# New states leave by transfers of single values, in place of transposes on TensorE with a staging buffer

## The reference

```
xn = rms_norm(x);  h, Bg, Cg, u, ga, gb = split(xn @ w_in)
conv_y, new_conv = causal_dwconv3(Cg * h, conv_buf)          # 512 channels
ssm_y, new_re, new_im = s5_mimo(u, s_re, s_im, ...)          # 32 groups x 64 complex states
x = x + (sigmoid(ga) * z_a + sigmoid(gb) * z_b) @ w_o
up_a, up_b = split(rms_norm(x) @ w_up)
up_a, new_ffn = causal_dwconv3(up_a, ffn_buf)                # 2816 channels
x = x + (gelu(up_a) * up_b) @ w_down
x = x + sigmoid(rms_norm(x) @ w_ple_gate) * (p @ w_ple);  y = rms_norm(x)
```

## Time and profile before

| | us |
|---|---|
| median of three runs (1610.47 to 1613.06) | 1612.05 |
| profiled execution, its own time | 1611.67 |
| its span, first to last instruction | 1609.9 |
| TensorE busy | 1553.1 |
| VectorE busy | 729.8 |
| ScalarE busy | 409.5 |
| GpSimd busy | 365.3 |

### The profile page before, as it was taken

One profiled execution on the slowest core, in us unless ns is written; L12 is line 12 of the kernel. 1 busy time (PEld: TensorE's weight loads), 2 busy tenths in 40 slices (PEclk: granted clock), 3 DMA queues, 4 the chain that ended last, 5 costly groups with the idle time before them and its releaser, 6 DMA issues.

```text
span 1609.9 us, 23664 instructions
## 1 busy us (share of the span) xinstructions
PE 1553.1 (96%) x9919; PEld 1536.0 (95%) x9919; DVE 729.8 (45%) x769; ACT 409.5 (25%) x466; POOL 365.3 (23%) x156
## 2 busy tenths in 40 slices
PE   7999997899999999999999999999999999989997
PEld 6989997899999999999999999999999999987996
DVE  4896797122222222234353444534344353447344
ACT  6302211243422232233121121211211112045113
POOL 1121220121211223433112131221303213054110
PEclk9899998999999999999999999999999999999999
DMA  6633526432211113232021020210202111020003
GB/s 179 200 86 92 82 53 171 108 85 70 76 40 50 52 39 107 91 105 74 5 78 52 26 65 13 78 52 27 65 13 78 39 39 52 26 66 14 27 23 119
DMA packets 165601, 109.48 MB, mean 68 GB/s; under 512 B 18192, under 2 KB 157116, under 8 KB 165486
## 3 DMA queue, kind: packets, MB, share of 16 engines
q1 hardware_dynamic: 158898, 100.25, 22.3%
q10 hardware_dynamic: 6656, 8.57, 1.6%
HBM read 90.21 MB, written 17.51 MB: 67 GB/s over the span
## 4 chain that ended last, share of the span: by engine, by line
PE 84%; DVE 7%; issue 5%; ACT 2%; DMA 1%; POOL 0%; SPq 0%; ACTq 0%; DVEq 0%; POOLq 0%
PE PS L1514 62%; PE PS L1784 16%; PE PS L1727 2%; DMA WST<-in_w_in 1%; DVE XL L1098 1%; PE PS L1677 1%; PE PS L1564 1%; POOL WL L603 0%; DVE ST L1206 0%; DVE ST L1207 0%; DVE XT L1418 0%; DVE OUTT L1493 0%; DVE S L1208 0%; DVE Q L1152 0%; DVE S L1210 0%
## 5 line engine op out<-in xcount | busy, mean ns | idle before, releaser
L603 POOL TENSOR_TENSOR WL<-WST,WH 128x1024 fp32r<-128x1024 f32 x108 | 261.7, 2424 | 1085.6 <-ACT WH L680 1085.6
L1514 PE MATMUL PS<-XH,WH 128*128 128x344 f32 x1920 | 409.8, 322 | 9.4 <-DVE TA L1117 3.9
L1514 PE MATMUL PS<-XL,WH 128*128 128x344 f32 x1920 | 408.9, 321 | 0.0
L1514 PE MATMUL PS<-XH,WL 128*128 128x344 f32 x1920 | 406.1, 320 | 0.0
L1514 PEld LDWEIGHTS PS<-XH,WH 128*128 128x128 f32 x1920 | 323.4, 188 | 11.1 <-issue 9.1
L1514 PEld LDWEIGHTS PS<-XL,WH 128*128 128x128 f32 x1920 | 326.2, 190 | 0.0
L1514 PEld LDWEIGHTS PS<-XH,WL 128*128 128x128 f32 x1920 | 321.0, 188 | 0.0
L680 ACT ACTIVATE WH<-WST 128x1024 fp32r<-128x1024 f32 x108 | 110.3, 1021 | 323.4 <-PE PS L1514 228.2
L1418 DVE TENSOR_TENSOR XT<-PS,XT 128x1032 f32<-128x1032 f32 x88 | 108.2, 1230 | 82.7 <-PE PS L1784 82.7
L1784 PE MATMUL PS<-GH,DHW 128*128 128x344 f32 x528 | 113.1, 323 | 5.4 <-DVE GL L1412 4.4
L1784 PE MATMUL PS<-GL,DHW 128*128 128x344 f32 x528 | 112.4, 321 | 0.0
(11 more groups left out here) (270 smaller groups left out, 1738.1 us busy)
## 6 DMA issues: line engine op xcount, KB each, us to landing
WST<-in_w_up SPq DMA_DIRECT2D x44, 512.0 KB, 3.9
WST<-in_w_in SPq DMA_DIRECT2D x32, 512.0 KB, 4.4
DST<-in_w_down SPq DMA_DIRECT2D x11, 1024.0 KB, 5.1
xscr<-XT SPq DMA_DIRECT2D x1, 4128.0 KB, 15.0
WST<-in_w_o SPq DMA_DIRECT2D x8, 512.0 KB, 4.4
WST<-in_w_ple_gate SPq DMA_DIRECT2D x8, 512.0 KB, 4.0
out_y_prompt<-OUTT SPq DMA_DIRECT2D x8, 512.0 KB, 2.9
XN<-in_x_prompt ACTq DMA_DIRECT2D x6, 512.0 KB, 8.5
```

What stands on the lines that cost most here:

```text
L603: nc.gpsimd.tensor_tensor(WL[:, w], WST[:, slot, 0:tiles * P], WH[:, w].bitcast(F32), ALU.subtract).then_inc(s_wl, 1)
L1514: last = mm(PS[:, 3 * (n % 2) + c, 0:TN], ww[:, w], xx[:, cols], start=(k == 0 and r == 0), stop=(k == ks - 1 and r == 2))
```

## The change

The 15 turns, the staging buffers OST and SST and SP's ten stores go. ScalarE issues transfers straight from FS and LAST to the outputs. One transfer fills one row of an output (one part of one batch entry), with the columns of FS or LAST as the source, so that every element is a piece of 4 bytes. 18 for the SSM and 10 for convolution A, with one plain copy of old rows from input to output, are issued behind `rms(1, N_A0)`; 10 for the FFN and one plain copy behind `gelu(FT - 1)`. The last wait of SP counts 40 transfers in place of 10.

```diff
@@ SP
-            sp.wait_ge(s_mf, M_OUT + 15)
-            sp.dma_start(out["conv_a_p"][0, 0], OST[0:2, 0:CA]).then_inc(s_so, 16)
...
-                sp.dma_start(out[f"ssm_{part}_p"][0].rearrange("b g p -> b (g p)"), half[0:1, :]).then_inc(s_so, 16)
-                sp.dma_start(out[f"ssm_{part}_s"][0].rearrange("b g p -> b (g p)"), half[1:1 + NB, :]).then_inc(s_so, 16)
...
-            sp.wait_ge(s_so, 160)
+            sp.wait_ge(s_so, 16 * (2 * (NB + 1) + 2 * (NB + 3)))
@@ ScalarE
             hi(G_P6, G_P6 % 2, N_A0)
             rms(1, N_A0)
 
+            for c, part in enumerate(("re", "im")):
+                rows = [out[f"ssm_{part}_p"][0, 0]] + [out[f"ssm_{part}_s"][0, b] for b in range(NB)]
+                for b, row in enumerate(rows):
+                    act.dma_start(row.rearrange("(j two) p -> (two p) j", two=2), FS[:, c, :, b],
+                                  allow_slow_non_contiguous=True).then_inc(s_so, 16)
+
+            def conv_states_out(name, kept, first, end):
+                rows = [out[name + "_p"][0, 0, k] for k in range(2)] + [out[name + "_s"][0, b, 1] for b in range(NB)]
+                for b, row in enumerate(rows):
+                    act.dma_start(row.rearrange("(t p) -> p t", p=P), LAST[:, first:end, b],
+                                  allow_slow_non_contiguous=True).then_inc(s_so, 16)
+                act.dma_start(out[name + "_s"][0, :, 0, :], a[kept][0, :, 1, :]).then_inc(s_so, 16)
+
+            conv_states_out("conv_a", "state_conv_a", 0, CT)
+
...
             gelu(FT - 1)
+            conv_states_out("ffn", "state_ffn_conv", CT, CT + FT)
             act.wait_ge(s_dst, FP * 16 + 16)
...
             hi(G_P7L, 0, N_PW0)
-            for k in range(4):
-                states_out(k)
             rms(2, N_P7)
-            for k in range(4, 15):
-                states_out(k)
@@ TensorE
-            for k in range(4):
-                states_out(k)
             sum_squares(N_P7, 2 * DT + 1)
-            for k in range(4, 8):
-                states_out(k)
             rms_read(2)
...
             down_out(N_PW0, N_PW0, 0, PH, PL, PHW, PLW)
-            for k in range(8, 15):
-                states_out(k)
...
-            pe.wait_ge(s_mf, M_OUT + 15)
+            pe.wait_ge(s_mf, M_PT + 5)
```

More of the change, by code:

```diff
@@ L88 @@
 M_PT = M_YO(CT)
-M_OUT = M_PT + 5
 def _stage_count(g, i=None, per_trip=0):
@@ L165, in decoder_step @@
         PL = at("PL", [P, PT * T], B0 + 6 * TB4, F32R)
-        SST = at("SST", [NB + 1, 2 * NJ * P], B0)
         AP = at("AP", [NJ, NPOW, P], C0)
@@ L191, in decoder_step @@
         PLW = at("PLW", [P, 2 * D], C0 + 16384, F32R)
-        OST = at("OST", [NB + 2, CA + FF], C0)
         XT = at("XT", [P, DT * T], D0)
@@ L977, in _ @@
                 split_hi(None, tile(XT, m), m, KV[:, K_PLE + m:K_PLE + m + 1], TC, DT + m + 1)
[L979 to L984, removed]
             def ple_gate(m, n):
```

## The result

The changed kernel takes 1838.03 us (median of 4 runs, 1820.08 to 1845.29), the kernel before 1611.26 (4 runs, 1609.39 to 1613.06). The ratio is 1.139, 95% interval 1.1305 to 1.1477: slower by 226.8 us. The forecast was slower by 68, with 1617 to 1775 as its range: right in sign, wrong by a factor of 3.3 in size, and the measured time lies outside the range. The profiled execution of the changed kernel took 1834.31 us, its span 1832.4. Its four runs lie 25 us apart, those of the kernel before 4.

A forecast was written before the change was run, and what follows sets the result against it. TensorE, busy 96%, was taken to bound the kernel, so holding up its inputs costs time. Stalls of 41.4 and 26.6 plus 1.6 for the clock less 1.2 for the turns gave +68.4 us: 1680 us, range 1617 to 1775.

The forecast's parts named there:

- The places: ScalarE held after the square root at 711.25 and the GELU ending at 1427.9; TensorE stalls 41.4 and 26.6 us.
- cover: Time ScalarE can be held before TensorE stalls: 8.3 us at the first place, 5.8 at the second.
- The price of a piece: Each 4-byte piece of the state stores takes a DMA engine 20 ns; ends 11.7 and 56.
- the middle of US: Source of the 20 ns: the store of US, 32 B pieces to HBM, estimated at 7 to 34 ns each.
- second rival: Pieces dearer, as many engines write 4 B into one short run: 40 to 56 ns, 1762 to 1828 us; 22%.
- WC's 56 ns: Price per piece from the WC transfers, 117.5% of 160 us over 3353 packets; upper end for the price.
- US and BN: Evidence against dear pieces: US's 32 B store at 34 ns at most; BN's 2048 pieces of 64 B, issued in 511 ns.
- The depth of the queue: ScalarE's queue, taken to be like SP's, still holds 140 pieces per engine when the last issue ends.
- The turns: After the FFN, removing them starts the next product 2.8 us sooner; clock restart costs 1.6, net 1.2 us gained.
- Traffic: Small pieces share DMA engines with weight loads, but a load has a product's time in hand, so no cost.
- The final wait: At the kernel's end: free, last piece leaves by 1463 us, 147 us before the end; up to 100 ns per piece.

The follow-up runs named there:

- values apart: Changed kernel with the same 38 transfers at the same places, but every value goes to scratch 640 B from the next; 1687.38 us, ratio 1.0476.
- the trials: Two kernels that store no states; in their place ScalarE issues nine trials of four transfers each at the first place; 32 B pieces took 10 ns.
- trial 2: In the kernel pricing pieces, without state stores: 4-byte stores to scratch, each partition's 16 to a run of its own; 41.5 us, 76 ns per piece.
- trial 0: In the kernel pricing pieces, without state stores: 4-byte stores to neighbouring places of one scratch row, as in the change; 36.2 us, 65 ns per piece.
- trial 1: In the kernel pricing pieces, without state stores: the same 4-byte pieces stored to scratch, each 640 B from the next; 12.4 us, 19 ns per piece.
- the first kernel that spread the rows: Changed kernel with its 38 transfers issued one at a time by SP between weight loads, none by ScalarE; 1621.39 us, ratio 1.0067 to the kernel before.

## Why the prediction was wrong

**The places, right.** TensorE's two waits stand where they were named, on WL and on GL, and each equals ScalarE's idle time less cover. First place: 143.5 - 8.3 = 135.2, measured 135.2. Second: 92.4 - 5.8 = 86.6 more than the old 4.4, so 91.0; measured 94.5. The missing 3.5 us are new: PHW and the last split are held together, so GpSimd makes PLW (1654.73, 4.50 us) while VectorE makes GL. VectorE and GpSimd there:

```profile
1655.64 4.69 DVE L1402 TENSOR_TENSOR GL<-TC,GH 128x1032 fp32r<-128x1032 f32 x1 [88.58 <-ACT GH L665]
```

```profile
1654.73 4.50 POOL L650 TENSOR_TENSOR PLW<-DST,PHW 128x2048 fp32r<-128x2048 f32 x1 [98.19 <-ACT PHW L665]
```

The same instruction took 1.23 us before, and 4.69 beside GpSimd's.

**The price of a piece: the step that failed.** The sum had 20 ns, "the middle of US, since that is the one small store to HBM". The packets that moved on ScalarE's queue can be counted. Changed kernel, windows 706 to 850.6 and 850.6 to 880 us (first place held, and what was left), then 1559 to 1652.6 and 1652.6 to 1700 (second place):

```profile
q10 hardware_dynamic: 41736, 0.17, 112.2%
q10 hardware_dynamic: 712, 0.02, 16.6%
q10 hardware_dynamic: 28104, 0.11, 138.9%
q10 hardware_dynamic: 232, 0.09, 5.2%
```

In the 144.6 us of the first place 2608 packets moved per engine, in the 93.4 of the second 1756: 55 and 53 ns each. With the values apart, in windows 710 to 764.7 and 1473 to 1507.2:

```profile
q10 hardware_dynamic: 42185, 0.17, 102.2%
q10 hardware_dynamic: 28021, 0.11, 114.6%
```

That is 2637 in 53.8 us and 1751 in 34.2, 20 ns each, just the forecast's price; and that kernel took 1687 us against the 1680 of the forecast. So the rows behind the 20 ns were not wrong for values that lie apart. What they lacked was the address: neighbours in one row of an output. US writes runs of 32 B, and such pieces cost 10 ns in the trials, with gaps or without. The second rival had the right price ("many engines write 4 B each into the same short run of a row") and, with WC's 56 ns, 1828 us; it was given 22%, and the range ended at 1775, near that rival's lower end of 1762. The argument against it was taken from US and BN, neither of which writes single values side by side. Its many engines are not needed, as trial 2 shows.

**The depth of the queue: no fixed number of pieces.** 140 per engine were assumed to be left when the last issue ends. By the same count of packets, in which one counts when it starts, 138 were left in trial 0 and 211 in trial 1, but only 45 at the first place (712 packets) and 15 at the second (232), where the last issue is the plain copy. So almost nothing was taken off the holds. That is 95 and 125 pieces more than the forecast held ScalarE for, at 55 and 53 ns together 12 us of the miss. It is also why the kernel with its values apart came out 18 us above its own expectation, which had taken off 250 where 16 and 20 were left. The count says when ScalarE is free, not when the values are there: trial 0 had started its last packet by 740 us and landed at 747.

**The turns, right in the first term, low in the second.** 2.8 us sooner and 1.6 lost to the clock, 1.2 net, were forecast. Measured in the changed kernel: 2.7 and 2.5, 0.15 net; without any stores 2.7 and 1.9.

**Traffic, right, with a gap.** A load has a product's time in hand almost everywhere, but not at the start of the FFN, where the first kernel that spread the rows lost 11 us. In the changed kernel that place was safe, since the pieces were in ScalarE's queue and came later. The final wait was free, as forecast: the last pieces had moved by 1700 us of 1832. (The margin given for it, 100 ns a piece, is 84 by the forecast's own figures; nothing hangs on it, as the hold moves the end of the kernel too.)

Sum with the measured terms: 135.2 for WL, 1.5 for the restart behind it, 94.5 - 4.4 = 90.1 for GL, less 0.15: 226.6 us. The spans of the two profiled executions differ by 222.5 only, but the changed kernel began the first FFN product 4.5 us sooner (708.24 against 712.71), in a stretch that the change does not touch; from there on it is 227.0. That the medians differ by 226.8 as well is in part luck.

## What to carry to other kernels

Before a transfer is cut into single values, count the pieces per DMA engine and look at where they land: at equal count the same transfers cost the kernel three times as much when the values were neighbours in HBM (227 us against 77). An engine that issues many such transfers in a row stands still until nearly all have moved (15 and 45 pieces per engine were left here of 1760 and 2624), so such transfers go one by one, on an engine whose stream has nothing urgent behind them, and never ahead of a load that is due. And a gap that must be there anyway is a free place for work on TensorE: taking the work out let the clock fall here and gave back almost nothing.

## What the runs showed of the hardware that was not expected

- In one execution each of the two kernels with trials, a 4-byte store to HBM took 76 ns per piece and engine with the next one 4 B on, 53 at 16 B, 42 at 32, 24 at 64 and 18 from 128 B up. A whole 32 B piece took 10 ns with or without gaps, 4-byte loads 8 ns, 4-byte copies within SBUF 7.
- A pause of 4.9 us brought TensorE's granted clock to an average of 0.56 over the next five microseconds and lengthened a product by 1.9 us; in the changed kernel the same pause cost 2.5. After the pause of 135 us the restart was shorter: groups of three matmuls of 1.22, 1.06, 1.06 and 0.78 us before they were at 0.64 again, 1.5 us in all.
- A VectorE subtraction of 128x1032 values took 4.69 us beside a GpSimd subtraction of 128x2048, where it took 1.23 with none beside it.
